# Expert weights of a mixture-of-experts kernel: one 1 MB transfer of 8 KB runs in place of two 512 KB transfers of 4 KB runs

## The reference

```python
g = jnp.einsum("nd,edf->nef", t, w_gate)
u = jnp.einsum("nd,edf->nef", t, w_up)
a = jax.nn.silu(g) * u * combine[:, :, None].astype(t.dtype)
y = jnp.einsum("nef,efd->nd", a, w_down)
```

## Time and profile before

| | |
|---|---|
| Time, median of 3 runs | 1002.31 us (998.33 to 1002.44) |
| Span of the profiled execution | 997.0 us |
| TensorE busy | 800.8 us, 80% of the span |
| SyncE's queue of transfers | 253.04 MB, 65.0% of 16 engines over the span |
| Issues from `w_gate`, `w_up`, `w_down` | 128 each, 512 KB each |

### The profile page before, as it was taken

How to read it: one execution, slowest core, us unless ns; L and a number is a source line. 1 busy time by engine, 2 the same in 40 slices (tenths; PEclk the granted TensorE clock), 3 DMA queues, 4 the chain that set the end, 5 groups by cost and what they waited for, 6 DMA issues and landing times.

```text
span 997.0 us, 19297 instructions
## 1 busy us (share of the span) xinstructions
PE 800.8 (80%) x7936; PEld 464.8 (47%) x7937; DVE 329.0 (33%) x894; ACT 195.6 (20%) x372; POOL 98.2 (10%) x109
## 2 busy tenths in 40 slices
PE   4158999970169999965999999999999999999750
PEld 0035668930039944534545455454553555545320
DVE  6149983699910002224021120211111121121116
ACT  0033316300230212210021120211111121121113
POOL 1020002067020010002000000000000000000000
PEclk8579999975579999986999999999999999999995
DMA  8910000440554570047999999999999999999924
GB/s 306 342 14 1 2 0 2 170 171 8 159 214 169 199 273 0 1 165 300 343 397 410 410 410 410 408 410 410 410 410 410 335 413 410 410 411 410 410 74 189
DMA packets 78154, 259.14 MB, mean 260 GB/s; under 512 B 19384, under 2 KB 19816, under 8 KB 73880
## 3 DMA queue, kind: packets, MB, share of 16 engines
q1 hardware_dynamic: 70840, 253.04, 65.0%
q10 hardware_dynamic: 5632, 2.18, 1.3%
q0 software_dynamic: 1632, 3.20, 0.9%
HBM read 252.49 MB, written 6.29 MB: 260 GB/s over the span
## 4 chain that ended last, share of the span: by engine, by line
issue 47%; DVE 3%; POOL 2%; DMA 2%; POOLq 1%; ACT 0%; SPq 0%; DVEq 0%
POOL y_scratch L495 1%; POOLq L513 1%; DMA slots<-slot_list 1%; DMA ring<-y_scratch 0%; DVE ring L1457 0%; DVE sreg L1446 0%; DVE sreg L1447 0%; POOL slot_list L469 0%; DVE sreg L1448 0%; POOL pool_tick L483 0%; DMA slot_list<-sreg,sloti 0%; DMA y_scratch<-vreg,sidx 0%; POOL sidx L488 0%; ACT sreg L723 0%; POOLq L512 0%
## 5 line engine op out<-in xcount | busy, mean ns | idle before, releaser
L995 PE MATMUL ps<-ring,vreg 128*32 128x512 f32 x2240 | 246.6, 599 | 14.1 <-issue 13.8
L995 PEld LDWEIGHTS ps<-ring,vreg 128*32 128x32 f32 x2240 | 74.6, 111 | 179.0 <-issue 179.0
L1017 PE MATMUL ps<-ring,vreg 128*32 128x256 f32 x2240 | 124.2, 380 | 17.0 <-ACT vreg L702 17.0
L1017 PEld LDWEIGHTS ps<-ring,vreg 128*32 128x32 f32 x2240 | 81.3, 110 | 56.0 <-issue 16.3
L745 PE MATMUL ps<-ring,silu_c 128*32 128x512 f32 x192 | 39.6, 925 | 72.8 <-DMA ring<-in_w_ada 72.8
L981 PEld LDWEIGHTS ps<-vreg,sreg 128*128 128x128 f32 x768 | 89.3, 196 | 14.2 <-issue 12.6
L981 PE MATMUL ps<-vreg,sreg 128*128 128x96 f32 x768 | 91.9, 281 | 1.5 <-DVE vreg L1378 1.5
L1408 DVE TENSOR_TENSOR vreg<-vreg,ps 128x256 f32<-128x256 f32 x48 | 17.4, 417 | 224.3 <-ACT vreg L697 224.3
L1418 DVE COPY vreg<-ps 32x256 f32<-32x256 f32 x96 | 40.7, 424 | 132.2 <-PE ps L1017 129.7
L954 PE MATMUL ps<-ring 128*128 128x512 f32 x192 | 83.1, 593 | 0.7 <-ACT ring L652 0.7
L709 ACT ACTIVATE vreg<-ps 32x256 f32<-32x256 f32 x96 | 35.9, 374 | 131.5 <-PE ps L1017 129.5
(11 more groups left out here) (257 smaller groups left out, 682.2 us busy)
## 6 DMA issues: line engine op xcount, KB each, us to landing
ring<-in_moe_w_gate SPq DMA_DIRECT2D x128, 512.0 KB, 11.8
ring<-in_moe_w_up SPq DMA_DIRECT2D x128, 512.0 KB, 13.2
ring<-in_moe_w_down SPq DMA_DIRECT2D x128, 512.0 KB
ring<-in_w_ada SPq DMA_DIRECT2D x24, 1024.0 KB, 8.8
ring<-in_ssm_w_glu SPq DMA_DIRECT2D x8, 1024.0 KB, 4.8
ring<-in_ssm_w_in SPq DMA_DIRECT2D x8, 512.0 KB, 12.5
ring<-y_scratch SPq DMA_DIRECT2D x6, 512.0 KB, 6.2
tmat<-ada_rows SPq DMA_DIRECT2D x4, 512.0 KB, 7.1
```

Source lines behind the costliest of these rows:

```text
L995: last = pe.matmul(ps[t][32 * j:32 * j + 32, :], xgT[:, k, 32 * t:32 * t + 32], w[:, :, 256 * j:256 * j + 256], start=(k == 0), stop=(k == ...
L1017: last = pe.matmul(ps[3 + t // 2][32 * dj:32 * dj + 32, 256 * (t % 2):256 * (t % 2) + 256], aT[:, t, c2, 32 * j:32 * j + 32], ring[:, KT + ...
```

## The change

Unit `2m` now holds 256 rows of `w_gate`, unit `2m+1` the same 256 rows of `w_up`, and a unit of `w_down` 256 rows of it. Partition `p` gets the neighbouring rows `2p` and `2p+1` of the 256, which are 8 KB in a row in DRAM, so one transfer of 1 MB fills a unit. What `k` stands for on the partitions changes with it: chunk `k` is now every second row. The gather reads its stationary operand from `h2` with a step of two elements, the transposes of `act_a` do so too, and TensorE waits for two units ahead of every second `k` and frees two after it. The number of matmuls, of loads and of bytes is the same.

```diff
             def load_unit(u, e):
-                if u < KT:
-                    for h, w in enumerate((w_gate, w_up)):
-                        sp.dma_start(ring[:, u, h * D:(h + 1) * D],
-                                     w[0, bass.ds(e, 1), u * P:(u + 1) * P, :].rearrange("a p n -> (a p) n")
-                                     ).then_inc(ld_unit[u], 16)
-                else:
-                    for h in range(2):
-                        k = 2 * (u - KT) + h
-                        sp.dma_start(ring[:, u, h * D:(h + 1) * D],
-                                     w_down[0, bass.ds(e, 1), k * P:(k + 1) * P, :].rearrange("a p n -> (a p) n")
-                                     ).then_inc(ld_unit[u], 16)
+
+                w, m = ((w_gate, w_up)[u % 2], u // 2) if u < KT else (w_down, u - KT)
+                sp.dma_start(ring[:, u, :], w[0, bass.ds(e, 1), 2 * P * m:2 * P * (m + 1), :].rearrange(
+                    "a (p c) n -> (a p) (c n)", c=2)).then_inc(ld_unit[u], 16)
...
-                        last = pe.matmul(bank[:, col * CAP:(col + 1) * CAP], h2[:, t, k * P:(k + 1) * P],
+                        first = 2 * P * (k // 2) + k % 2
+                        last = pe.matmul(bank[:, col * CAP:(col + 1) * CAP], h2[:, t, first:first + 2 * P - 1:2],
                                          onehot[:, t, :], start=(t == 0), stop=(t == NT - 1))
...
-                    pe.wait_ge(ld_unit[k], it * 32 + 32)
-                    w = ring[:, k, :].rearrange("p (a n) -> p a n", a=2)
+                    m, c2 = divmod(k, 2)
+                    if c2 == 0:
+                        pe.wait_ge(ld_unit[2 * m], it * 16 + 16)
+                        pe.wait_ge(ld_unit[2 * m + 1], it * 16 + 16)
+                    w = ring[:, 2 * m:2 * m + 2, c2 * D:(c2 + 1) * D]
...
-                    last.then_inc(unit_free, 1)
+                    if c2 == 1:
+                        last.then_inc(unit_free, 2)
...
-                        last = pe.transpose(out, act_a[:, t, c2 * P:(c2 + 1) * P], ident[:])
+                        last = pe.transpose(out, act_a[:, t, c2:c2 + 2 * P - 1:2], ident[:])
...
-                        pe.wait_ge(ld_unit[KT + j], it * 32 + 32)
+                        pe.wait_ge(ld_unit[KT + j], it * 16 + 16)
```

## The result

The changed kernel takes 1005.73 us (median of 15 runs, 1002.99 to 1009.68); the kernel before, in as many runs beside it, 999.35 us (997.81 to 1003.27). The ratio is 1.006, with a 95% interval of 1.0045 to 1.0075: slower by 6 us. The forecast was no change. The time lies in the forecast range of 994 to 1010, but the loss is real, and slower had 0.20 of the chance.

What follows compares the result with a forecast made beforehand. PE was taken to set the pace, never waiting for a weight in the loop. The terms summed to 0 + 0 + 0 = 0 on the median of 1002.3 us, giving 1002 us, range 994 to 1010.

Steps and rivals of the forecast that it cites:

- What bounds the kernel: Expert loop: PE sets the pace and waits for no weight; the 5.80 us stall is a fetch of code.
- The transfers: Weight stream: 1 MB issues raise it from 410 to 426 GB/s, 17 us less transfer time, worth nothing on the path.
- The waits: PE's waits for two units ahead of each second `k`: cost nothing, from 0 to 1.7 us.
- The step of two in the gather: PE's 768 loads of `h2` in the gathers: cost taken as 0, with 0 and 88 us as ends.
- reading 1: Gather loads: a 16-byte piece takes as long as two elements, so a step of two costs 0.
- readings 2 and 3: Gather loads: a surcharge per piece, 38 ns a load, 29 us; or any step costs double, 88 us. Chance 0.17 together.
- The transposes: 70 loads of `act_a` with a step of two: 0, 18 or 55 ns each; taken as 0.
- The stall: Ahead of the last expert: the code fetch stays; floor 0, at most 5.8 us more.
- Rival D: Last expert: the code fetch gets longer behind 8 KB packets, up to 5.8 us, 1003 to 1008 us; chance 0.06.
- C: Last expert: the stall is late weights, and the faster stream removes it: 7.1 us, 995 us; chance 0.07.
- The sum: Whole kernel: 0 + 0 + 0 = 0 on top of the runs' median, 1002 us.
- rival A: Whole kernel: no change, PE's pieces stay 13.94, 5.60 and 7.11 us; 1002 us, range 997 to 1007; chance 0.70.

Runs made afterwards that it cites:

- the thin stream: The kernel before with only 128 of 1024 columns of each expert row brought in, TensorE's work unchanged; 992.37 us in one run.
- every loss taken back: Changed kernel with VectorE writing `h2` and `act_a` in the new order, TensorE reading without a step, one wait for a pair; 1001.13 us, ratio 1.0006.

## Why the prediction was wrong

*What bounds the kernel.* Right. PE sets the pace, no weight is late, and the stall ahead of the last expert is a fetch of code: the thin stream left 3.13 us of it, and keeping the expert in the loop took it away, together with the packet of code. That 17 us less transfer time would be hidden was right as well: the change without its steps is at 1.0003, and with every loss taken back at 1.0006.

*The transfers.* 426 GB/s forecast, 422 measured.

*The waits.* "Cost: nothing, from 0 to 1.7 us" was a price for data that comes late, and none came late. The cost that did come was another one, and it has no term in the prediction: the second wait itself, at the head of an expert, takes 0.09 to 0.10 us, 1.2 to 1.4 us over the 14 turns. The three other pairs of waits in an expert cost nothing, the gate piece stays at 13.94 us. That the one at the head costs because PE has nothing queued there is argued and not shown.

*The step of two in the gather.* This is the step that failed, and the largest term: "I take reading 1, cost 0". Of the three readings the first was right, as the runs with three, four and eight elements show; readings 2 and 3, to which I gave 0.17, were wrong by factors of 6 and 19. But reading 1 gives only the part that goes with the columns, and I took the rest as 0. It is 6 ns a load, just under the 6.5 ns that the text named as the point from which the step alone decides. 720 loads of the 15 gathers in the loop by 6.2 ns are 4.4 us.

*The transposes.* Taken as 0; the loads grew by 69 ns, more than the 55 that I had as the upper end, and of this 0.05 us an expert reached the path: 0.8 us. I had also misread. From 141 to 196 ns is a factor of 1.4 and 0.43 ns a column, not "close to an even two", and the pace of these transposes hardly changed, as the timeline of the kernel before shows, with the step of 16 first:

```profile
68.17 1.06 PE L782 MATMUL ps<-ident,vreg 128*128 128x128 f32 x8
...
82.73 1.04 PE L782 MATMUL ps<-ident,vreg 128*128 128x128 f32 x8
```

So the length of one load is no price for a transpose. Only L819 bore out the doubling.

*The stall.* "It stays": 5.92 us for 5.80. Rival D fell, and C. That 1005.73 us lies in D's span of 1003 to 1008 is chance.

*The sum.* 4.4 + 0.8 + 1.4 = 6.6 us where I had 0; the loop shows 6.55 and the runs 6.4. The level that the sum was put on was high by chance: the three first runs of the kernel before had a median of 1002.31 us, fifteen have 999.35. Nor do 5.3 us lie around the span: in the 15 runs of the changed kernel it is 1.7 to 1.9 us each, and the profiled execution of the kernel before, with its span of 997.0 us, was among the shorter ones. The time lies even in rival A's own range of 997 to 1007, but that range stood for the spread of the runs and not for a cost on PE's path. Three terms that I each rounded to nothing lie on one side, because each of them could only cost: the forecast had a gain that was excluded (the stream) and small losses on the path. With that, a forecast of a small loss was the one to make, and 0.20 for slower was too little.

## What to carry to other kernels

When a change speeds up a transfer that nobody waits for, its side effects on the bounding engine are all that is left of it: price those to the nanosecond and multiply by their count, since 6 ns by 720 loads and 0.1 us by 14 turns were nearly the whole result. A layout that suits the DMA is best paid for on an engine that has time to spare, here VectorE's write and not TensorE's read; look there too for the one place where it has none, which cost 1.3 us ahead of the router. And look at the last turn of a loop: the code that stands behind it cost 0.8% of the time, no less than the change did.

## What the runs showed of the hardware that I had not expected

A load of 128 fp32 columns behaved as if paced by 16-byte pieces: for load and matmul 117 ns without a step, 123 with two elements, 178 with three, 240 with four and 245 with eight. The Trainium skill's page "SBUF — State Buffer" ("Door 1: The DMA port swizzle") has the rule of two hits on a 16-byte line, and the runs follow it to within 6 ns with two elements and 12 ns with eight. The same passage puts the step that is free at up to 4 fp32; here the step of four took twice as long. The transposes' loads grew from 141 to 210 ns with two elements to a piece, which the rule does not give, while four of these transposes took 0.65 us in place of 0.60.

TensorE stood still 5.8 us for the code behind its loop with the DMA engines full of weights, 3.1 us with them at 60 GB/s, and 0.3 us when there was no such code. From the packet of code to TensorE's start it was 2.7 to 2.9 us, with the engines full and nearly idle; with them full the packet came 2.6 us later. A second wait, for a transfer that was not late, cost TensorE 0.1 us at the head of an expert.
